# Sample attention with 32 stationary columns per matmul, neighbouring matmuls on different strips of 32 output rows

## The reference, cut to what matters

```python
def diff_attn_sample(q, k_past, v_past, k_new, v_new, lam):
    ...
    p = (probs(q1, kp1, kn1) - lam * probs(q2, kp2, kn2)).astype(v_new.dtype)
    return (jnp.einsum('bhqk,bkhe->bqhe', p[..., :p_len], v_past)
            + jnp.einsum('bhqk,bkhe->bqhe', p[..., p_len:], v_new))
```

## Time and profile before

| | |
|---|---|
| median of 3 runs | 1470.77 us |
| lowest and highest run | 1462.28 and 1472.52 us |
| span of the profiled execution, first to last instruction | 1465.0 us |
| mean granted TensorE clock in it | 0.912 of full speed |
| PE busy | 1253.8 us, 86% of the span |
| DVE, ACT, POOL busy | 916.1, 698.6 and 252.7 us |

### The profile page before, as it was taken

One profiled execution on the slowest core, in us unless ns is written; L12 is line 12 of the kernel. 1 busy time (PEld: TensorE's weight loads), 2 busy tenths in 40 slices (PEclk: granted clock), 3 DMA queues, 4 the chain that ended last, 5 costly groups with the idle time before them and its releaser, 6 DMA issues.

```text
span 1465.0 us, 16900 instructions
## 1 busy us (share of the span) xinstructions
PE 1253.8 (86%) x5888; PEld 963.9 (66%) x5888; DVE 916.1 (63%) x1112; ACT 698.6 (48%) x748; POOL 252.7 (17%) x261
## 2 busy tenths in 40 slices
PE   5989994599999996299999999989937999999930
PEld 4766764478888885277776666657736788888820
DVE  4256357498888885832321444464675988888836
ACT  4233223277777775222112544432224777777721
POOL 2021020241111121410000000000302411112314
PEclk9999995699999998599999999969858999999975
DMA  9302047269999996732230133213462899999842
GB/s 341 122 29 93 1 173 285 84 224 359 374 372 372 376 368 214 296 116 92 89 116 1 59 116 115 78 48 118 187 238 83 302 376 373 369 375 371 299 181 77
DMA packets 142529, 302.56 MB, mean 207 GB/s; under 512 B 11888, under 2 KB 12048, under 8 KB 142352
## 3 DMA queue, kind: packets, MB, share of 16 engines
q1 hardware_dynamic: 123024, 250.23, 47.9%
q0 software_dynamic: 19168, 51.31, 9.8%
q10 hardware_dynamic: 288, 0.36, 0.1%
HBM read 288.36 MB, written 30.28 MB: 217 GB/s over the span
## 4 chain that ended last, share of the span: by engine, by line
PE 78%; DVE 13%; DMA 3%; ACT 3%; issue 2%; POOLq 0%; POOL 0%; SPq 0%; DVEq 0%; ACTq 0%
PE ps L1422 20%; PE ps L1424 20%; PE ps L1423 20%; PE ps L1657 3%; DVE wl L868 2%; PE ps L1720 2%; PE ps L1705 2%; PE ps L1581 2%; DVE x L1225 2%; PE ps L1467 2%; ACT wh L617 2%; PE ps L1674 1%; PE ps L1691 1%; DMA xg<-x_rows,gcur 1%; DMA yl<-y_rows 1%
## 5 line engine op out<-in xcount | busy, mean ns | idle before, releaser
L868 DVE TENSOR_TENSOR wl<-raw,wh 128x2048 fp32r<-128x2048 f32 x210 | 481.0, 2314 | 221.3 <-ACT wh L617 217.4
L617 ACT ACTIVATE wh<-raw 128x2048 fp32r<-128x2048 f32 x210 | 398.4, 1915 | 202.0 <-PE ps L1424 138.0
L1422 PE MATMUL ps<-wh,xTh 128*128 128x512 f32 (+1 forms) x560 | 227.7, 407 | 22.8 <-DVE wl L868 14.8
L1424 PE MATMUL ps<-wh,xTl 128*128 128x512 f32 (+1 forms) x560 | 223.0, 398 | 0.0
L1423 PE MATMUL ps<-wl,xTh 128*128 128x512 f32 (+1 forms) x560 | 223.0, 398 | 0.0
L1422 PE MATMUL ps<-wh,xgTh 128*128 128x512 f32 x512 | 209.3, 409 | 6.7 <-DVE xgTl L1175 5.7
L1423 PE MATMUL ps<-wl,xgTh 128*128 128x512 f32 x512 | 203.9, 398 | 0.0
L1424 PE MATMUL ps<-wh,xgTl 128*128 128x512 f32 x512 | 203.5, 398 | 0.0
L1422 PEld LDWEIGHTS ps<-wh,xTh 128*128 128x128 f32 (+1 forms) x560 | 98.6, 176 | 58.9 <-issue 22.5
L1422 PEld LDWEIGHTS ps<-wh,xgTh 128*128 128x128 f32 x512 | 97.3, 190 | 36.2 <-DVE wl L868 8.3
L1424 PEld LDWEIGHTS ps<-wh,xTl 128*128 128x128 f32 (+1 forms) x560 | 98.0, 175 | 34.2
(11 more groups left out here) (258 smaller groups left out, 1641.1 us busy)
## 6 DMA issues: line engine op xcount, KB each, us to landing
raw<-in_moe_w_up SPq DMA_DIRECT2D x120, 1024.0 KB, 10.5
raw<-in_moe_w_down SPq DMA_DIRECT2D x62, 1024.0 KB, 11.7
raw<-in_a_w_in SPq DMA_DIRECT2D x8, 1024.0 KB, 16.7
ahead_up<-in_moe_w_up SPq DMA_DIRECT2D x8, 1024.0 KB, 8.7
yl<-y_rows POOLq DMA_DIRECT2D x8, 1024.0 KB, 8.4
raw<-in_cache_k SPq DMA_DIRECT2D x16, 512.0 KB, 3.8
raw<-in_cache_v SPq DMA_DIRECT2D x16, 512.0 KB, 4.9
raw<-in_a_w_out SPq DMA_DIRECT2D x4, 1024.0 KB, 5.1
```

The lines of the kernel that those rows point to most:

```text
L617: act.activation(wh[:, slot], src, ACT.Copy).then_inc(high[key], 1)
L868: dve.tensor_tensor(wl[:, slot], src, wh[:, slot].bitcast(F32), ALU.subtract).then_inc(low[key], 1)
L1422: pe.matmul(out, high_, w_high, start=start, stop=False)
L1424: return pe.matmul(out, low_, w_high, start=False, stop=stop)
```

## The change: 32 stationary columns, four strips

Sample scores: each matmul now has only the 32 columns of `qpad` that hold its queries and writes only the strip of 32 rows in which they fall. A strip belongs to one sequence and four heads, so that four matmuls in a row write four different strips; four such rounds make the 16 matmuls. A round needs the keys of both sequences, so the 16 now stand in two bursts of eight at j = 4 and j = 5, instead of four bursts of four at j = 2 to 5. The number of matmuls, passes and moving columns is unchanged. The semaphore `sm_s` rises once a group instead of twice, and its readers count accordingly.

Sample values: head h now writes strip h % 4 of one bank, columns by h // 4, so that eight heads go through the strips 0, 1, 2, 3, 0, 1, 2, 3. The eight matmuls for the new rows follow the same rule. Four ACT copies of 32 x 256, one for each strip, replace the one of 32 x 1024, and `sm_o` counts to 4.

```diff
-            act.activation(o[4][0:NSAMP], ps[0:NSAMP, 6:8].rearrange("p a n -> p (a n)"), ACT.Copy).then_inc(sm_o, 1)
+            for j in range(4):
+                act.activation(o[4][0:NSAMP].rearrange("p (a j e) -> p j a e", j=4, e=P)[:, j],
+                               ps[32 * j:32 * j + 32, 6, 0:2 * P].rearrange("p (a e) -> p a e", e=P), ACT.Copy
+                               ).then_inc(sm_o, 1)
...
-                for h in range(4 * half, 4 * half + 4):
-                    lhs = qpad[:, (b2 * 8 + h) * P:(b2 * 8 + h + 1) * P]
-                    mm = pe.matmul(ps[:, 5, 0:2 * P + NSAMP], lhs, kts[:, b2, h], start=(b2 == 0 and h == 0),
-                                   stop=(b2 == 1 and h == HEADS - 1), skip_group_check=True)
-                if half:
+                for i in range(2 * part, 2 * part + 2):
+                    for strip in range(4):
+                        b2, h, rows = strip // 2, strip % 2 * 4 + i, slice(32 * strip, 32 * strip + 32)
+                        at = (b2 * 8 + h) * P + 32 * strip
+                        mm = pe.matmul(ps[rows, 5, 0:2 * P + NSAMP], qpad[:, at:at + 32], kts[:, b2, h],
+                                       start=(i == 0), stop=(i == 3), skip_group_check=True)
+                if part:
                     mm.then_inc(sm_s, 1)
...
+            def sample_o(h):
+
+                return ps[32 * (h % 4):32 * (h % 4) + 32, 6, h // 4 * P:(h // 4 + 1) * P]
+
...
-                    mm = pe.matmul(ps[0:NSAMP, 6 + h // 4, h % 4 * P:(h % 4 + 1) * P], ptz[:, page, b2, h],
-                                   vals[:, page, h * P:(h + 1) * P],
-                                   start=(g == 0 and b2 == 0 and page == 0 and h % 4 == 0), stop=False,
+                    mm = pe.matmul(sample_o(h), ptz[:, page, b2, h], vals[:, page, h * P:(h + 1) * P],
+                                   start=(g == 0 and b2 == 0 and page == 0 and h < 4), stop=False,
                                    skip_group_check=True)
...
-                    if 2 <= j < 6:
-                        sample_scores(g, (j - 2) // 2, (j - 2) % 2)
+                    if j in (2, 4):
+                        keys_turned(g, (j - 2) // 2)
+                    if 4 <= j < 6:
+                        sample_scores(g, j - 4)
```

More of the change, by code:

```diff
@@ L589, in _ @@
             pool.wait_ge(park_out, 16 * TILES)
-            pool.wait_ge(sm_o, 1)
+            pool.wait_ge(sm_o, 4)
             pool.wait_ge(at_o, 4 * HEADS)
@@ L808, in keys_copy @@
                 act.wait_ge(sm_kt, 8 * g + hk + 1)
-                after(act, sm_s, 2 * (g - 1) + b2 + 1)
+                after(act, sm_s, g)
                 act.activation(kts[:, b2, 4 * half:4 * half + 4, page * P:(page + 1) * P],
@@ L1298, in queries @@
                 dve.wait_ge(qpad_zero, 1)
-                after(dve, sm_s, 2 * g)
+                after(dve, sm_s, g)
                 for b2 in range(2):
@@ L1309, in sample_max @@
             def sample_max(g):
-                dve.wait_ge(sm_s, 2 * g + 2)
+                dve.wait_ge(sm_s, g + 1)
                 new = ps[:, 5, 256:288]
@@ L1400, in _ @@
             turn_low(T_O + 2, subg)
-            dve.wait_ge(sm_o, 1)
+            dve.wait_ge(sm_o, 4)
             squares(4)
@@ L1692, in turn_keys, with keys_turned, sample_scores @@
                 mm.then_inc(sm_kt, 1)
[L1694 to L1702, removed]
-                for h in range(4 * half, 4 * half + 4):
-                    lhs = qpad[:, (b2 * 8 + h) * P:(b2 * 8 + h + 1) * P]
-                    mm = pe.matmul(ps[:, 5, 0:2 * P + NSAMP], lhs, kts[:, b2, h], start=(b2 == 0 and h == 0),
-                                   stop=(b2 == 1 and h == HEADS - 1), skip_group_check=True)
-                if half:
+            def keys_turned(g, b2):
+                pe.wait_ge(sm_ktc, 8 * g + 4 * b2 + 4)
+                pe.sem_inc(keys_used, 1)
+            def sample_scores(g, part):
+                if part == 0:
+                    pe.wait_ge(new_keys, 2)
+                    pe.wait_ge(sm_q, g + 1)
+                    after(pe, sm_ptz, g)
+                for i in range(2 * part, 2 * part + 2):
[5 more added lines that the diff above has]
+                if part:
                     mm.then_inc(sm_s, 1)
@@ L1759, in _ @@
             for h in range(HEADS):
-                mm = pe.matmul(ps[0:NSAMP, 6 + h // 4, h % 4 * P:(h % 4 + 1) * P], ptn[:, h],
-                               x[0:NSAMP, 4, h * P:(h + 1) * P], start=False, stop=(h % 4 == 3), skip_group_check=True)
+                mm = pe.matmul(sample_o(h), ptn[:, h], x[0:NSAMP, 4, h * P:(h + 1) * P], start=False, stop=(h >= 4),
+                               skip_group_check=True)
             mm.then_inc(sm_pv, 1)
-            pe.wait_ge(sm_o, 1)
+            pe.wait_ge(sm_o, 4)
             def turn_o(t):
```

## The result

The changed kernel takes 1430.12 us (median of 4 runs, 1429.88 to 1431.42), the kernel before 1471.64 us in the same call (4 runs, 1462.28 to 1473.16). The ratio is 0.973, 95% interval 0.9705 to 0.9757. The forecast was 1451 us with a range from 1440 to 1472: the direction was right, and the gain of 41.5 us is a little over twice the 19.5 us of the sum. The profiled execution after took 1430.12 us, with a span of 1428.3 us; the span before was 1465.0.

A forecast was written before the change was run, and what follows sets the result against it. PE was taken to bound the loop. Values 7.8 plus scores 12.6, less shape changes 1.0 and waits 2.1, gave 17.3 us; with 2.2 behind the loop, 19.5 off 1470.8 made 1451 us, range 1440 to 1472.

The forecast's parts named there:

- two-deep overlap: Score and value bursts: each matmul costs one pass instead of two, plus one pass per burst; 1451 us, chance 0.57.
- no overlap: Rival 1: strips are worked off one after the other, so nothing is saved; 1473 us, chance 0.15.
- changes of shape: Loop: eight score bursts now pay 0.12 us each when PE goes from 128-column transposes to 32 columns; 1.0 us lost.
- values in the loop, twelve bursts: Loop: each burst of 16 value passes falls from 1.76 to 1.11 us; 7.8 us saved.
- waits that come out: Loop: PE waits 0.27 us for P in each of eight steps that lose scores; 2.1 us lost, bounds 0 and 4.
- behind the loop: After the loop: value passes end 4 to 5 us earlier, but DVE's weight split caps the gain at 2.5; 2.2 taken.
- What a pass costs: PE bursts: value passes start 0.11 us apart, score passes 0.243 us; both go by their moving columns.
- exposed load: Bursts: the next strip's weight load stands between passes, 0.03 us (0 if hidden, 0.015 taken); total saving then 17 us.
- The median: Whole run: the profiled span, 1465.0, lies 5.8 us under the median of 1470.77; the median moves by the full 19.5 us.
- emptying: Rival 2: PE empties at each change of strip, 0.12 us per matmul, 25 us lost; 1495 us, chance 0.10.
- Deeper overlap: Rival 3: passes of three strips or more run together, bursts fall to 1/2.4, 29 us saved; 1442 us, chance 0.06.
- The clock case: Rival 4: overlap works, but PE idles and its clock falls inside the loop, costing 10 us; 1461 us, chance 0.12.

The follow-up runs named there:

- neighbours on one strip: Changed kernel with its matmuls reordered so that two neighbours at a time share a strip, same passes and strips; 1434.39 us, ratio 0.9765.
- with two strips: Changed kernel with the values and new rows on two strips (head h to strip h % 2) instead of four, scores unchanged; 1438.11 us, one run.
- The kernel with the squares spread: Changed kernel with DVE's squares of finished heads in half-tile pieces over more steps of the loop; 1430.48 us, ratio 0.9725 to the kernel before.

## Why the prediction was wrong

**The step that failed** is this one: "Passes are issued in the order of the program, so the overlap is two deep: a matmul costs one pass instead of two". The first passes of the strips do start in the order of the program, 7 or 13 ns apart, but not all passes do: one that must wait for its strip doesn't hold up those behind it for other strips, so the overlap is four deep, one pass for each strip. A value burst takes 0.58 us to the next work on PE where the forecast's two-deep overlap gave 1.11. The kernels with neighbours on one strip and with two strips show the cause: the burst goes by the passes per strip and not by their order. There was no row with two strips. I knew the ends (no overlap, a quarter), and put the value between them by a single queue that I had inferred from a trace with one strip, where a queue for each strip looks the same.

| term | forecast, us | measured, us | |
|---|---|---|---|
| scores, eight bursts, with the changes of shape | 11.6 | 22.2 | 4 x 5.55, group 1 |
| values in the loop, twelve bursts | 7.8 | 15.4 | 3 x 5.14, group 1 |
| waits that come out | -2.1 | -5.6 | what the loop lacks to the two above |
| loop | 17.3 | 32.0 | |
| last step to the last P result | 0 | 2.65 | |
| behind the loop | 2.2 | 2.6 | |
| outside, start and rest together | 0 | -0.5 | |
| sum | 19.5 | 36.7 | |

- **What a pass costs** was right. With 0.243 us for a score pass and a quarter of the passes in a row, a group's scores save 32 x 0.243 - 8 x 0.243 = 5.83 us, less two changes of shape of 0.12: 5.59 against the measured 5.55 to 5.57. A value burst saves 12 x 0.11 = 1.32; measured 5.14 / 4 = 1.29. So the price of a change of shape fits, and no exposed load is needed.
- **Waits that come out**: waits for P grew by 3.7 us, inside the bounds of 0 to 4 but nearly twice the 2.1 charged, and the fall of the clock behind one of them cost 1.5. Together that is 5.2 of the 5.6. I charged the waits to the eight steps that lost their scores. Six of the eight got none; the waits grew for the P of steps 19, 21 and 27 (by 1.9, 0.8 and 0.8 us), and in all three DVE has squares to do. The kernel with the squares spread shows this: 3.5 us come back in the loop, the fall's among them.
- **Last step to the last P result**: forecast at nothing. Before, the clock was 0.51 in that stretch; after, it fell only at 931.0 and the stretch has 0.75. The kernel before, profiled again, has 10.6 us and 0.75 there too. So it is where the clock happens to fall, not the change.
- **Behind the loop** the cap by DVE was right in cause and nearly in size (2.5 us at most, measured 2.6), and holds although PE's part shrank by 7.7 us.
- **The median** was to move as the profile does. It moved by 4.8 us more; stretches at half clock in the loop, which other executions of before have and its profile here had not, can account for that. The 5.8 us by which the prediction has its profile under the median set a span against a time; in the changed kernel the time is 1.8 us above the span (1430.12 and 1428.3), so 4.0 are left.
- **The rivals.** No overlap and emptying fall with the length of the bursts; a change of strip leaves 7 ns between two passes, where emptying was to cost 0.12 us. Deeper overlap came true, and its 29 us still fell short, with 1/2.4 for the burst instead of 1/3.2. It had a chance of 0.06 on the one argument that two passes of a strip stand in a row; with both ends equally supported by the rows it should have had as much as the two-deep case. The clock case came true in part: 3.4 us at 0.50, worth 1.5 us.

## What to carry to other kernels

The small float32 matmuls of this kernel run side by side when they write different strips of 32 output rows, in both orders tried. For others like them, count the passes of the fullest strip, and don't put a price between two bounds by a mechanism that the trace at hand can't tell from its rival. When a stream shrinks by a fifth, look in each step for what another engine does ahead of the next input, since that is where most of the new waits came out here. A gain of some us in one stage can vanish at a meeting point of two engines far behind it: cut the spans of both traces at the same instructions, and compare their clocks, before calling an edit useless.

## What was not expected of the hardware

A DVE operation with two inputs from SBUF (2.29 us) that began 0.16 to 0.44 us ahead of an indirect gather on POOL stretched its issue from 1.08 to 2.8 to 3.1 us and the time to its data from 4.2 to 8.1 to 8.4; begun 0.04 us behind, it did nothing to it. In both delayed cases the issue ends 0.95 to 0.97 us after DVE's end (263.44 and 264.41, 1059.13 and 1060.08).

The Trainium skill, SBUF — State Buffer, section SBUF: two separate sides, says that DVE and GpSimd share a pair of ports as an exclusive lock, which the one that starts first holds for its whole instruction; a DVE operation with two SBUF inputs takes part only against a GpSimd operation that reads SBUF. The trace agrees as to the issue, whose row names `gcur`, the rows to gather, as an input: begun behind the split, it ends only 0.95 to 0.97 us after it. The trace shows no block the other way: the split that began 0.04 us behind the issue lasts 2.29 us like the others. Nor does the lock account for all: from the end of the issue to PE's first use 3.2 us pass in the undelayed case and 5.3 in the delayed ones, and where these 2.1 us come from stays open.
